# Reordering the seven-product stretches of three feed-forward layers in an fp32 transformer kernel

## The reference, cut to what matters

```python
def _swiglu(h, w_gate, w_up, w_down):
    return (jax.nn.silu(h @ w_gate) * (h @ w_up)) @ w_down
...
h = h + _swiglu(_rmsnorm(h, norm_ffn[layer]), w_gate[layer], w_up[layer], w_down[layer])
...
ff = (jax.nn.silu(u @ w_ffn_gate[l]) * (u @ w_ffn_up[l])) @ w_ffn_down[l]
```

## Time and profile before

| | us |
|---|---|
| median of 3 runs | 1931.07 |
| lowest, highest | 1929.42, 1934.48 |
| profiled execution, its own time | 1928.26 |
| profiled execution, span | 1926.5 |
| PE busy in the span | 1875.2 |
| DVE busy, ACT busy | 1232.3, 1000.2 |
| span less the busy time of PE | 51.3 |

### The profile page before, as it was taken

One profiled execution on the slowest core, in us unless ns is written; L12 is line 12 of the kernel. 1 busy time (PEld: TensorE's weight loads), 2 busy tenths in 40 slices (PEclk: granted clock), 3 DMA queues, 4 the chain that ended last, 5 costly groups with the idle time before them and its releaser, 6 DMA issues.

```text
span 1926.5 us, 27817 instructions
## 1 busy us (share of the span) xinstructions
PE 1875.2 (97%) x10276; PEld 1581.5 (82%) x10276; DVE 1232.3 (64%) x1864; ACT 1000.2 (52%) x1748; POOL 198.1 (10%) x203
## 2 busy tenths in 40 slices
PE   7999999999999899999999999999999999999997
PEld 5778778998888677777999888778888789988886
DVE  5566557785366766755888446688767787763322
ACT  5556545554377544445555357765555555552222
POOL 0000020110021100001111002210111101100000
PEclk9999999999999999999999999999999999999999
DMA  4122124663365322222565245521121135643331
GB/s 139 66 65 65 44 77 121 158 157 102 104 207 197 132 88 87 87 66 92 155 149 153 88 146 188 183 102 67 71 72 66 63 99 144 161 116 95 91 99 64
DMA packets 72069, 213.07 MB, mean 111 GB/s; under 512 B 8864, under 2 KB 9376, under 8 KB 71968
## 3 DMA queue, kind: packets, MB, share of 16 engines
q1 hardware_dynamic: 52800, 163.47, 25.5%
q0 software_dynamic: 18064, 46.67, 10.6%
q10 hardware_dynamic: 1104, 1.58, 0.2%
HBM read 205.39 MB, written 2.10 MB: 108 GB/s over the span
## 4 chain that ended last, share of the span: by engine, by line
PE 83%; DVE 7%; ACT 5%; issue 3%; DMA 2%; SPq 0%; DVEq 0%; ACTq 0%; POOLq 0%
PE ps L403 19%; PE ps L405 18%; PE ps L404 18%; PE ps L1041 5%; PE ps L1043 5%; PE ps L1042 5%; PE ps L2844 1%; DVE wlo L385 1%; PE ps L2709 1%; PE ps L1660 1%; PE ps L2690 1%; PE ps L2725 1%; PE ps L1685 1%; ACT whi L374 1%; PE ps L1675 1%
## 5 line engine op out<-in xcount | busy, mean ns | idle before, releaser
L403 PE MATMUL ps<-xh,whi 128*128 128x512 f32 x960 | 384.4, 400 | 7.1 <-DVE wlo L385 3.6
L404 PE MATMUL ps<-xl,whi 128*128 128x512 f32 x960 | 376.7, 392 | 0.0
L405 PE MATMUL ps<-xh,wlo 128*128 128x512 f32 x960 | 376.7, 392 | 0.0
L385 DVE TENSOR_TENSOR wlo<-raw,whi 128x1024 fp32r<-128x1024 f32 (+1 forms) x224 | 283.2, 1268 | 142.3 <-ACT whi L374 140.4
L374 ACT ACTIVATE whi<-raw 128x1024 fp32r<-128x1024 f32 (+1 forms) x232 | 235.5, 1027 | 118.5 <-PE ps L405 118.4
L403 PEld LDWEIGHTS ps<-xh,whi 128*128 128x128 f32 x960 | 182.5, 190 | 49.9 <-issue 7.3
L405 PEld LDWEIGHTS ps<-xh,wlo 128*128 128x128 f32 x960 | 181.9, 190 | 39.0
L404 PEld LDWEIGHTS ps<-xl,whi 128*128 128x128 f32 x960 | 182.3, 190 | 38.2 <-issue 1.9
L403 PE MATMUL ps<-acth,whi 128*128 128x512 f32 x528 | 210.5, 399 | 0.0
L404 PE MATMUL ps<-actl,whi 128*128 128x512 f32 x528 | 205.9, 390 | 0.0
L405 PE MATMUL ps<-acth,wlo 128*128 128x512 f32 x528 | 205.7, 390 | 0.0
(11 more groups left out here) (388 smaller groups left out, 3604.0 us busy)
## 6 DMA issues: line engine op xcount, KB each, us to landing
raw<-in_gu SPq DMA_DIRECT2D x96, 512.0 KB, 3.4
raw<-in_down SPq DMA_DIRECT2D x48, 512.0 KB, 3.8
raw<-in_qkv SPq DMA_DIRECT2D x24, 512.0 KB, 4.2
wada<-in_ada POOLq DMA_DIRECT2D x24, 512.0 KB, 3.5
tmps<-in_ada POOLq DMA_DIRECT2D x24, 512.0 KB, 3.7
raw<-in_qkvb SPq DMA_DIRECT2D x24, 512.0 KB, 3.7
raw<-in_gu SPq DMA_DIRECT2D x36, 256.0 KB, 4.3
raw<-in_gu POOLq DMA_DIRECT2D x36, 256.0 KB, 4.1
```

Source lines behind the costliest of these rows:

```text
L385: eng.tensor_tensor(wlo[:, s, 0:n], raw[:, s, 0:n], whi[:, s, 0:n].bitcast(F32), ALU.subtract).then_inc(lo_done, 1)
L403: pe.matmul(ps[:, bank], whi[:, s, w], hi[:, k0 + k], start=start and k == 0, stop=False)
L404: pe.matmul(ps[:, bank], whi[:, s, w], lo[:, k0 + k], start=False, stop=False)
L405: mm = pe.matmul(ps[:, bank], wlo[:, s, w], hi[:, k0 + k], start=False, stop=stop and k == n - 1)
```

## The change

It makes five moves and removes or adds no computation:

1. PE: the first ordinary unit of group PRE (`standard_pe(..., units=(0,))`) and the three waits are issued ahead of `fourth(11)`; the units 1 to 3 follow.
2. ACT in a pair: `hidden_hi(i - 1, ...)` comes first, ahead of the split of "last"; `silu(i, 0)` comes behind the split of "direct".
3. DVE in a pair: `hidden_lo(i - 1, ...)` comes ahead of the split of "last" in place of behind that of "direct".
4. DVE at the entry: `split_lo(u, (1, 0))` comes ahead of the first two token sums.
5. ACT in gu0: the activation that makes `csil` comes behind `ffn_act` in place of ahead of it.

```diff
@@ fast_act
                 bank_a, bank_b, bank_c = fast_banks(p)
+                if i:
+                    hidden_hi(i - 1, p % 2)
                 if p:
                     fast_hi(act, u, x, "last", p)
...
                     standard_hidden(act, f, PRE - 1, 1)
-                if p % 2:
-                    silu(i, 0)
-                    if i:
-                        hidden_hi(i - 1, 1)
-                elif i:
-                    hidden_hi(i - 1, 0)
                 if final:
                     wait(act, x.mm, mm_count(2, p))
                     split_hi(act, u, (PRE, 0))
                 else:
                     fast_hi(act, u, x, "direct", p + 1)
+                if p % 2:
+                    silu(i, 0)
                 wait(act, x.mm, mm_count(5, p))
@@ fast_dve
                 if p:
                     inner(p - 1)
+                if i:
+                    hidden_lo(i - 1, p % 2)
+                if p:
                     fast_lo(dve, x, "last", p)
...
                     fast_lo(dve, x, "direct", p + 1)
-                if i:
-                    hidden_lo(i - 1, p % 2)
                 if final:
                     restore_lo(dve, x)
@@ fast_pe
-        def fast_pe(pe, x):
+        def fast_pe(pe, x, behind):
...
-            fourth(FAST_PAIRS - 1)
             wait(pe, x.last, FAST_PAIRS - 1)
             wait(pe, x.outer, x.steps(FAST_PAIRS - 3) + 1)
             wait(pe, x.token_lo, 8)
+            behind()
+            fourth(FAST_PAIRS - 1)
@@ ffn_dve
             tile(0, 0, raw)
+            split_lo(dve, u, (1, 0))
             fast_token(dve, x, 0)
             fast_token(dve, x, 1)
-            split_lo(dve, u, (1, 0))
             fast_token(dve, x, 2)
@@ standard_pe
-        def standard_pe(pe, u, f, t, ready=None, ready_at=0, behind_first=None):
+        def standard_pe(pe, u, f, t, ready=None, ready_at=0, behind_first=None, units=range(4)):
 
-            for j in range(4):
+            for j in units:
@@ ffn_pe, and the same in raw_ffn_pe
-            fast_pe(pe, x)
-            with pe.Fori(PRE, u.count) as t:
+            fast_pe(pe, x, lambda: standard_pe(pe, u, f, PRE, units=(0,)))
+            standard_pe(pe, u, f, PRE, units=(1, 2, 3))
+            with pe.Fori(PRE + 1, u.count) as t:
                 standard_pe(pe, u, f, t)
@@ ACT's program, gu0
             res_act(act, U["o_a"], r0a, "ffn0", begun=1)
+            ffn_act(act, U["gu0"], f0, fast["gu0"])
             act.activation(csil, column("c", 0, KT), ACT.Silu).then_inc(set_a, 1)
-            ffn_act(act, U["gu0"], f0, fast["gu0"])
             act.preload_act_table_set(EXP_LN)
             act.wait_ge(set_a, 3)
```

## The result

The changed kernel takes 1914.61 us (median of 5 runs, 1912.80 to 1922.17) against 1931.07 before: a ratio of 0.9918, interval 0.9898 to 0.9939. It is faster, as forecast, but by 15.8 to 16.5 us (over all executions, and by these medians) and not by 8.8.

What follows compares the result with a forecast made beforehand. PE's stream of matmuls, with some 50 us of holes, bounds the kernel. Gains of 15.7 less losses of 6.9 net 8.8 us: 1928.26 becomes 1919.5, or 1922.3 us from the median 1931.07; range 1917.3 to 1928.3.

Steps and rivals of the forecast that it cites:

- gu2's entry: Entry of the gu2 stretch: lists no wait like those at gu0 and gu1, so gains nothing.
- The exit: Exits of the three stretches: PE's waits for L947 go, 7.5 us gained, and 1.7 for the clock fall in gu2.
- The pairs: Inside pairs: waits for snapshots L918 and L924 go, 3.5 us gained; a new wait in ten odd pairs loses 1.7.
- the chain: Odd pairs of gu0 and gu1: product, L872, split of "last", snapshot 1 end about 0.07 us late; 0.17 lost per pair.
- The entries: Entries of gu0 and gu1: waits of 1.34, 0.50 and 0.42 us go with restarts, 3.0 us gained.
- `csil`: Start of down0: PE waits at L2750 until ACT makes `csil`, 3.5 us lost, and 1.7 for a clock fall.
- The clock: 1.7 us gained as the fall behind gu2's exit goes, 1.7 lost to a fall behind the hole at down0.
- the first rival: Boundary wait at three exits and snapshot chain in ten odd pairs: gain shrinks to 3.0, 1928.1 us; chance 0.25.
- the slower one: Snapshot 1 held by ACT's queue head in all 30 gated pairs: 1941.6 us at 0.7 per pair; chance 0.05.
- The third: No clock fall at L2750 and snapshot 1 in time in odd pairs: 3.4 less, 1918.9 us; chance 0.10.

Runs made afterwards that it cites:

- pairs_alone: Moves 2 and 3 on the kernel before, without the move of `silu(i, 0)` and the lines taken out: 1925.11 us, ratio 0.997.
- no_pairs: Moves 1 and 4 alone on the kernel before, no move inside the pairs and `csil` in front: 1917.8 us, ratio 0.9924.
- csil_in_front: The changed kernel with move 5 undone, `csil` back ahead of `ffn_act`: 1913.43 us, ratio 0.9918 to the kernel before.
- snapshot_first: csil_in_front with snapshot 1 ahead of the split of "last" on ACT: 1913.82 us, ratio 0.991 to the kernel before.
- entry_alone: Move 4 alone on the kernel before: 1928.82 us, ratio 0.9982.
- csil_front_2: csil_in_front, unchanged, measured once more: 1913.38 us, ratio 0.9902 to the kernel before.
- csil_alone: Move 5 alone on the kernel before: 1934.25 us, ratio 1.0016.
- no_gate: The changed kernel without PE's wait for the third `set_a` ahead of down0: 1914.7 us, ratio 0.9894 to the kernel before.
- all_three: The changed kernel without PE's `set_a` wait and with snapshot 1 ahead of the split of "last": 1910.36 us, ratio 0.9895 to the kernel before.

## Why the prediction was wrong

Two steps failed: what moves 2 and 3 bring inside the pairs was priced too low, and gu2's entry was put at nothing. The other terms were near.

**The exit (7.5 and 1.7, measured 9.3): right.** The corner behind 24 matmuls of 512 columns, as the forecast drew it, no wait, and no wait for unit 2. The sizes held; the reading of the clock term did not: instead of one sure fall in gu2, 6 of 12 exit holes of 2.2 us had a fall behind them in the four profiles of kernels with the old exit and old pairs (1, 3, 1 and 1 of 3), at 1.7 each some 2.6 per execution. None of the three shorter holes of pairs_alone had one, nor any of the 27 exits without a hole.

**The pairs (3.5 less 1.7): this step failed.** The forecast had a net gain of 1.8, and the runs show 4.0 ± 1.7 (no_pairs against csil_in_front). The holes inside pairs are the time from a stretch's first matmul to the last one ahead of the corner of pair 11, less the same in snapshot_first, summed over the three stretches. In six profiles with the old order they come to 4.5, 5.8, 5.0, 5.0, 5.8 and 5.9 (mean 5.3), and in five with the new order to 1.3 to 1.5. (Left out are 1.8 in entry_alone and 0.4 in csil_front_2, both in pair 0 and ended by nothing that the profile shows.) pairs_alone, a sixth with the new order, has 3.2 through its wait for L898. Two things were off.

The loss was a little smaller than forecast. In odd pairs from 3 to 11 of gu0 and gu1 the restart costs 0.03 + 0.10 = 0.13, so 10 x 0.13 = 1.3, and there is none in gu2. The changed kernel shows it in pair 7 (timeline):

```profile
392.84 0.69 DVE L977 SCALAR_TENSOR_TENSOR tmps<-tmps,sqsum 128x512 f32<-128x512 f32 x1
...
393.56 0.63 ACT L872 ACTIVATE acth<-tmps 128x512 fp32r<-128x512 f32 x1 [2.95 <-DVE tmps L977]
...
395.04 0.37 ACT L898 ACTIVATE tmps<-ps 128x256 f32<-128x256 f32 x1
395.31 0.28 PE L1042 MATMUL ps<-xh,wlo 128*128 128x256 f32 x1
395.46 0.39 PE L1040 MATMUL ps<-token_hi,whi 128*128 128x256 f32 x1
395.68 0.28 PE L1041 MATMUL ps<-token_lo,whi 128*128 128x256 f32 x1
```

Product, rounding and snapshot follow each other as the chain said (0.72 and 1.48 between starts), the block starts 0.15 behind the matmul ahead of it in place of 0.12 and its first matmul takes 0.39 and holds the next one up by 0.10. The forecast of the mechanism and of its place was right; snapshot_first confirms it.

The gain was the larger error, in two parts. The forecast priced the four listed waits at 3.5, while the starts of that same profile's matmuls hold 4.5 inside pairs, since a wait that is satisfied just in time is not listed. And 4.5 is the lowest of the six. Four of the other five list a wait for snapshot 1 of 0.4 to 0.9 in pair 2 or 3 of gu0, each behind a split of "last" that waited for its transfer, and there are more waits for snapshots 2 and 3. In the new order the waits for snapshots 2 and 3 are gone in every profile. Those for snapshot 1 are gone in all but pairs_alone; why the transfers land in time in the others was not tested.

**The entries (3.0): right in gu0 and gu1, wrong in gu2.** 41.67 to 39.34 and 40.15 to 39.34 is 3.1. For gu2 the forecast said that its entry "lists no such wait and gains nothing". That held for the one profile it read, where the clock fell on the units ahead and PE came late enough to find the split made. csil_alone, with the same code in gu2, has no fall there, and its DVE and PE show the wait:

```profile
1574.86 1.22 DVE L785 TENSOR_TENSOR token_raw<-whole 128x1024 f32<-128x1024 f32 x1
...
1577.33 1.22 DVE L385 TENSOR_TENSOR wlo<-raw,whi 128x1024 fp32r<-128x1024 f32 x1
...
1578.70 0.47 PE L403 MATMUL ps<-xh,whi 128*128 128x512 f32 x1 [1.99 <-DVE wlo L385]
```

These are the low part behind two token sums that move 4 turns round. The windows from the entry's first matmul to the first of this unit, in the kernel before and then in csil_alone, and in the changed kernel:

```profile
1558.93:1576.63 17.70, 17.70 (x82) 14.99 (x80) 15.62 (x24) 13.26 (x19) 0.00 (x0) 0.81 0.00 0
1561.32:1578.70 17.38, 15.18 (x82) 12.28 (x80) 15.29 (x24) 13.31 (x19) 0.00 (x0) 1.00 0.00 0
1552.78:1568.89 16.11, 16.11 (x81) 13.72 (x80) 13.87 (x22) 13.27 (x19) 0.00 (x0) 0.89 0.01 2
```

At a clock of 0.81 and at 1.00 the old order takes nearly the same time, once with no wait and once with 1.99. Over the profiles, gu2's entry is 39.46, 39.45, 39.25, 40.83 and 39.26 in the five without move 4 (mean 39.7; the waits 0, 0, 1.12, 1.99 and 1.99), and 37.1 to 37.9 in eight of the nine with it, 39.5 in the ninth, where the clock was low for 6.8 us; no wait in any of them (mean 38.0). So move 4 is worth some 1.7 more than forecast. This is read from traces; entry_alone's 3.5 ± 2.5 agrees with the 4.1 of all three entries, but also with 2.4.

**`csil` (3.5 and 1.7): the hole right, the clock nearly.** 3.11 listed, 3.27 in starts, with 3.4 forecast. The clock fell behind it in 2 of 3 profiles, so 1.1 on average. Behind the holes of 2.2 us at the exits it fell in 6 of 12. By the rule of the Trainium skill ("TensorE: Matmul & The Clock Gate", Why this matters for your kernels), that idle gaps between bursts of matmuls bring the clock back to its low level, the fall behind the hole at down0 is sure; measured, it is a tendency.

**The clock (0 net): 1.5 placed, and no more shown.** The falls that could be placed give 2.6 - 1.1 = 1.5 less of cost, and the table has 4.0 ± 2.1 (95%). The seven kernels with neither an exit hole nor the hole at down0 (38 executions) have a cost of 14.5, 3.2 ± 1.2 under before, which the 2.6 of the exits nearly makes up. The changed kernel should stand above these by its hole at down0 and stands at 13.7, within its own scatter. At the other places where the clock falls (about 17, 251, 652 to 672, 857, 1261 to 1301 and 1551 to 1578 us) the profiles with the old exit and with the new one are as long at the low level, 18.4 and 18.6 us on average (five and nine of them).

**The sum again.** With the sizes found, 7.5 + 2.6 for the exits, 3.9 for the pairs, 4.8 for the entries, less 3.3 and 1.1 for `csil`, it comes to 14.4. The 15.8 ± 2.0 of the executions is not to be told from that. Of the 5.6 that this sum has more than the forecast, the pairs are 2.1, gu2's entry 1.7, the exits' clock 0.9, `csil` 0.8 and gu0's and gu1's entries 0.1.

**One profiled execution had to stand for all.** The forecast took 1928.26 less 8.8 and moved it to the median of three runs. The mean of 66 executions is 1931.3, so the sum's starting point was good, but its terms were those of an execution 3 us faster than usual. Its holes inside pairs were the smallest of six, and its low clock hid the wait in gu2's entry.

**The rivals.** No wait for L385 held unit 2 and none for the snapshots is listed in even pairs of the changed kernel, so neither the first rival (1928.1) nor the slower one (1941.6) is seen in it; the slower one's mechanism, a late split of "last" that holds snapshot 1, stands once in pairs_alone. The third, no loss at L2750 and in the odd pairs, had a time nearer to the result (1918.9), but not the right mechanism: both losses were there. Two numbers of the forecast do not follow from its own terms: the slower rival turns the sign at (8.8 + 1.7) / 30 = 0.35 per pair and not at 0.3, since 1.7 was already counted, and the first rival's time is 1928.1 and not the 1928.3 of the range. Neither touches the forecast time.

**The parts.** By the ratios: exit 9.3, pairs 5.8, entries 3.5, less 3.1 for move 5: 15.5 in sum, of which 1.7 is counted twice (in exit and pairs), so 13.8, and 15.8 and 15.4 for all together. The difference lies within the intervals of the parts. Move 5 makes a hole of 3.3 for 0.7 to 1.6 at the entry as long as PE waits for it, and its gain at the entry stays once that wait is dropped (no_gate, all_three).

## What to carry to other kernels

Where a reordering is to remove many waits of a few tenths of a microsecond, take several profiles of the same kernel first: the listed waits of one profile gave 3.5 here for holes that average 5.3. Before a place is put at nothing because it lists no wait, look at the clock ahead of it: in gu2's entry a low clock had hidden a wait of up to 1.99. Before work that increments a semaphore is moved behind long work, look at every waiter on that count, and ask of each whether it needs it at all; here the one costly waiter did not. Price a fall of the clock behind a hole as a chance, not as never or always; here it came behind 8 of 15 holes of 2.2 to 3.1 us.

## What was not expected of the hardware

The clock falls at other places from one execution to the next. At 251 us, ahead of all changed code, it fell in seven of the fourteen profiles and not in the other seven, over kernels that are the same up to there. The mean granted clock of the kernel before went from 0.986 to 0.995 in 23 executions on one chip; the one at 0.995 took 1926.03 us, the nine at 0.989 and 0.990 took 1929.04 to 1935.65, but the one at 0.986 took 1931.94. So a part of the spread of its times is clock, and the clock alone does not set it.

A fall of the clock can cost next to nothing. In gu2's entry of the old order, 6.8 us at the low level made the stage 39.46 against 39.26 without a fall, because a wait of 1.99 went away.

One execution of no_gate took 4656.57 us, with the other five between 1907.91 and 1914.95; nothing explains it, and it did not come back in all_three, which has the same edit.

A listed wait is not what it costs. A wait of 2.25 cost 2.41 and a slower first matmul; and a semaphore that comes just in time, which the profile doesn't list at all, cost 0.13 in the odd pairs.
